# Sums over channels of a LayerNorm in four 32-column groups, with smaller edits at the start and in a scan

## What is computed

```python
# first block, at its very start: the modulation of the input from c
mod = jnp.dot(jax.nn.silu(c), w_mod[l]) + b_mod[l]          # 1 x 6144
h = rms_norm(x, g_norm1[l]) * (1.0 + scale1) + shift1
proj = jnp.dot(h, w_in[l])

# second block, Conformer branch: a LayerNorm over 1024 channels
u = causal_depthwise_conv(u, conf_conv_w[i], conf_conv_b[i])   # 31 taps
u = jax.nn.silu(layer_norm(u, conf_ln_g[i], conf_ln_b[i]))
y_conf = u * jax.nn.silu(cgate)

# second block, state-space branch: a scan over chunks of 128 tokens
def step(h, inp):
    s, d = inp                     # d: decay of the chunk
    return h * d[..., None, None] + s, h
```

## Time and profile before

| | |
|---|---|
| three runs | 2256.68, 2260.80, 2262.57 us; median 2260.8 |
| the profiled execution | 2260.23 us, of which its span is 2258.5 |
| busy shares of the span | PE 93%, PE weight loads 72%, DVE 76%, ACT 47%, POOL 8% |
| mean granted clock of PE | 0.96 of full speed |
| moved by DMA | 381.7 MB, mean 169 GB/s |

### The profile page before, as it was taken

One profiled execution on the slowest core, in us unless ns is written; L12 is line 12 of the kernel. 1 busy time (PEld: TensorE's weight loads), 2 busy tenths in 40 slices (PEclk: granted clock), 3 DMA queues, 4 the chain that ended last, 5 costly groups with the idle time before them and its releaser, 6 DMA issues. The chain is left out here.

```text
span 2258.5 us, 24881 instructions
## 1 busy us (share of the span) xinstructions
PE 2095.7 (93%) x9816; PEld 1619.0 (72%) x9816; DVE 1710.6 (76%) x1731; ACT 1064.4 (47%) x1213; POOL 178.5 (8%) x152
## 2 busy tenths in 40 slices
PE   5999998999945999999999869999999988899998
PEld 3766844777834888888888557888888764588876
DVE  4565248895566899999999469999999858883776
ACT  4288134883214777777777322113132156524043
POOL 2000010000000011111111200000000000024040
PEclk8999998999967999999999979999999998999999
DMA  9111161002286899999998931121123143253111
GB/s 335 48 38 38 38 240 55 1 1 86 112 318 237 314 402 394 398 397 393 402 393 310 291 123 40 66 80 42 47 86 136 40 165 124 81 194 127 38 66 66
DMA packets 130014, 381.71 MB, mean 169 GB/s; under 512 B 10579, under 2 KB 21099, under 8 KB 129920
## 3 DMA queue, kind: packets, MB, share of 16 engines
q1 hardware_dynamic: 115104, 340.41, 39.6%
q0 software_dynamic: 7568, 23.09, 4.0%
q10 hardware_dynamic: 7248, 16.93, 1.9%
HBM read 337.28 MB, written 43.06 MB: 168 GB/s over the span
## 5 line engine op out<-in xcount | busy, mean ns | idle before, releaser
L2269 DVE SCALAR_TENSOR_TENSOR arena<-arena,vecs 128x1023 f32<-128x1023 f32 (+14 forms) x240 | 304.3, 1268 | 7.1
L1702 DVE TENSOR_TENSOR w_low<-W,w_high 128x2048 fp32r<-128x2048 f32 x96 | 216.9, 2286 | 38.8 <-ACT w_high L1647 38.8
L1971 PE MATMUL Q<-hT_high,w_high 128*128 128x512 f32 (+1 forms) x736 | 230.7, 393 | 1.3 <-PEq L1991 1.3
L1702 DVE TENSOR_TENSOR w_low<-arena,w_high 128x2048 fp32r<-128x2048 f32 x96 | 218.3, 2289 | 17.4 <-ACT w_high L1647 17.4
L1647 ACT ACTIVATE w_high<-W 128x2048 fp32r<-128x2048 f32 x96 | 184.0, 1919 | 96.1 <-PE Q L1577 65.2
L1971 PE MATMUL Q<-hT_low,w_high 128*128 128x512 f32 (+1 forms) x720 | 225.4, 391 | 0.0
L1971 PE MATMUL Q<-hT_high,ring_low 128*128 128x512 f32 x704 | 220.6, 391 | 0.0
L1647 ACT ACTIVATE w_high<-arena 128x2048 fp32r<-128x2048 f32 x96 | 184.2, 1920 | 74.5 <-PE Q L1577 74.5
L1577 PE MATMUL Q<-w_high,x_high 128*128 128x512 f32 x512 | 160.6, 395 | 2.4 <-DVE x_low L1705 2.4
L1984 ACT ACTIVATE w_high<-W 128x1024 fp32r<-128x1024 f32 x44 | 46.4, 1057 | 244.4 <-PE Q L1971 242.0
L1971 PEld LDWEIGHTS Q<-hT_high,w_high 128*128 128x128 f32 (+1 forms) x736 | 136.0, 185 | 34.1 <-issue 2.4
(11 more groups left out here) (449 smaller groups left out, 4160.2 us busy)
## 6 DMA issues: line engine op xcount, KB each, us to landing
W<-in_w_dram SPq DMA_DIRECT2D x48, 2048.0 KB, 13.3
arena<-in_w_dram SPq DMA_DIRECT2D x48, 2048.0 KB, 12.1
W<-in_w_mod_dram SPq DMA_DIRECT2D x12, 2048.0 KB, 15.7
W<-in_w_in_dram SPq DMA_DIRECT2D x12, 2048.0 KB, 9.1
W<-in_w_out_dram SPq DMA_DIRECT2D x6, 2048.0 KB, 9.9
spill<-arena ACTq DMA_DIRECT2D x24, 512.0 KB, 2.6
W<-in_w_in_dram SPq DMA_DIRECT2D x8, 1024.0 KB, 8.7
W<-cs_rows SPq DMA_DIRECT2D x11, 512.0 KB, 3.6
```

What stands on the lines that cost most here:

```text
L1702: nc.vector.tensor_tensor(wl[:], chunk_src(r, j), wh[:].bitcast(F32), ALU.subtract).then_inc(low_v, 1)
L1971: ins = nc.tensor.matmul(Q[rows, 2 * pair_of(n) + half, :], w[:, k], x[:, k, HALF * half:HALF * half + HALF], start=k == 0 and w is high a ...
L2269: ins = nc.vector.scalar_tensor_tensor(conf[:, i, j:], u[:, 0:S - j], w, conf[:, i, j:], ALU.mult, ALU.add)
```

## The change

1. c is loaded as 8 rows of 128 beside the other rows; one transpose of 32 rows (in the place of 24) turns all into columns and comes ahead of the product of unit 0. ACT reads c's columns from PSUM for the silu. `small_loads` moves from the first block's POOL list to that of the next block. The 16 matmuls that make columns are cut into four groups of four, each behind the product of the unit after.
2. `mean` and `var` become two entries each. Entry 0: 16 matmuls of 32 columns of ones, tile k to the 32-partition group k mod 4, so each group holds the sum over two tiles. ACT copies the pair to SBUF (`group_part`). Entry 1: two matmuls (one for each half) with the full ones, which add the groups; every group holds its sum 32 times, so the scales are 1/(32 * 1024). The mean moves behind z4, the variance behind z5. The squares get eight buffers instead of two, and no wait for PE.
3. `decay_of(i)` has four places, and waits for the update of step i-4.
4. xs is loaded in three DMAs of 128, 384 and 512 tokens; PE waits for the second at chunk 1 and for the third at chunk 4.

```diff
-                act.dma_start(c_col, A["c"][0].rearrange("(k p) -> p k", p=P), allow_slow_non_contiguous=True).then_inc(c_in, 16)
+                act.dma_start(row_stack[3 * KD:], A["c"][0].rearrange("(k p) -> k p", p=P)).then_inc(row_in, 16)
...
-                act.wait_ge(c_in, 16)
-                nc.scalar.activation(silu_c, c_col, ACT.Silu).then_inc(c_ready, 1)
+                act.wait_ge(row_tr, 1)
+                nc.scalar.activation(silu_c, Q[:, 7, 3 * KD:4 * KD], ACT.Silu).then_inc(c_ready, 1)
...
+                def turn_part(u):
+                    pe.wait_ge(mod_copied, u + 1)
+                    for j in range(4 * u, 4 * u + 4):
...
-                pe.wait_ge(row_in, 32)
+                pe.wait_ge(row_in, 48)
+                nc.tensor.transpose(Q[:, 7, 0:4 * KD], row_stack, ident[0:4 * KD, 0:4 * KD]).then_inc(row_tr, 1)
...
                     mod_product(pe, unit(pe, u), 4 + u % 2)
+                    turn_part(u - 1)
+                turn_part(3).then_inc(cols_mm, 1)
...
-        order.insert(order.index(("z", 4)), ("mean", 0))
-        order.insert(order.index(("z", 5)), ("var", 0))
+        at_z5 = order.index(("z", 5))
+        order[at_z5:at_z5] = [("mean", 0), ("mean", 1)]
+        at_z6 = order.index(("z", 6))
+        order[at_z6:at_z6] = [("var", 0), ("var", 1)]
...
-                for n, cols_n in enumerate((slice(0, 2 * P), slice(2 * P, S))):
+                for n, cols_n in enumerate((slice(0, P), slice(P, 4 * P), slice(4 * P, S))):
...
+                        if m == 0:
...
+                            pe.wait_ge(ready, KD)
+                            for half in range(2):
+                                for k in range(KD):
+                                    g = k % GROUPS
+                                    ins = nc.tensor.matmul(Q[P // 4 * g:P // 4 * g + P // 4, 2 * pair_of(n) + half, :],
+                                                           ones[:, 0:P // 4],
+                                                           terms[k][:, HALF * half:HALF * half + HALF],
+                                                           start=k < GROUPS, stop=k >= GROUPS)
+                        else:
+                            pe.wait_ge(in2_s, s_level[kind, 0])
...
+                                                       group_part[:, HALF * half:HALF * half + HALF],
...
-                        if k >= 2:
-                            act.wait_ge(sq_used, k - 1)
-                        nc.scalar.activation(conf_sq[k % 2], conf[:, k], ACT.Square).then_inc(sq_ready2, 1)
+                        nc.scalar.activation(conf_sq[k], conf[:, k], ACT.Square).then_inc(sq_ready2, 1)
...
+                    elif kind in ("mean", "var") and m == 0:
+                        ins = nc.scalar.activation(group_part, pair(what), ACT.Copy)
...
-                    if i >= 2:
-                        act.wait_ge(state_ready, i - 1)
+                    if i >= 4:
+                        act.wait_ge(state_ready, i - 3)
```

More of the change, by code:

```diff
@@ L187, in program @@
         skip_col = small_cols(KD)
-        chunk_decay = small_cols(2 * HPG)
+        chunk_decay = small_cols(4 * HPG)
         mv = small_cols(2)
@@ L524, in _ @@
                 send_units(sync, U_GATE1 + NU)
+            @block.gpsimd
+            def _(pool):
+                small_loads(pool)
             @block.tensor
@@ L1860, in program @@
         place = {what: n for n, what in enumerate(order)}
-        vector_reads = [w for w in order if w[0] in ("value", "mean", "turn", "bc", "xs")]
+        vector_reads = [w for w in order if w[0] in ("value", "turn", "bc", "xs") or w == ("mean", 1)]
         chunks = [w for w in order if w[0] not in ("mean", "var", "turn")]
@@ L1875, in program @@
                     act_list.append(("step", chunks[p]))
-        act_list.insert(act_list.index(("high", chunks.index(("z", 7)))), ("step", ("var", 0)))
+        at_z7 = act_list.index(("high", chunks.index(("z", 7))))
+        act_list[at_z7:at_z7] = [("step", ("mean", 0)), ("step", ("var", 0)), ("step", ("var", 1))]
         scalar_steps = [what for kind, what in act_list if kind == "step"]
@@ L1924, in program @@
         decayed = [spare2[:, 0], tiles(2), spare[:, 0]]
+        conf_sq = [tiles(0), tiles(1), tiles(3), tiles(5), tiles(37)] + [spare2[:, j] for j in (0, 2, 3)]
         cs_bc = [spare2[:, 1], tiles(3), spare[:, 1]]
@@ L1932, in program @@
         grown = arena[:, 37 * 1024 + 768:37 * 1024 + 896]
-        xs_in = [sem(f"xs_in{n}") for n in range(2)]
+        xs_in = [sem(f"xs_in{n}") for n in range(3)]
         cs_in = [sem(f"cs_in{j}") for j in range(3)]
@@ L2154, in _ @@
                         continue
[L2155 to L2157 removed]
+                    if kind in ("mean", "var"):
+                        if m == 0:
+                            terms, ready = ([conf[:, k] for k in range(KD)], conf_ready) if kind == "mean" else \
+                                (conf_sq, sq_ready2)
+                            pe.wait_ge(ready, KD)
[8 more added lines that the diff above has]
+                            pe.wait_ge(in2_s, s_level[kind, 0])
                             for half in range(2):
                                 ins = nc.tensor.matmul(Q[:, 2 * pair_of(n) + half, :], ones[:],
[L2160 to L2165, removed]
[L2166 to L2172 removed]
+                                                       group_part[:, HALF * half:HALF * half + HALF],
+                                                       start=True, stop=True)
                         ins.then_inc(in2_mm, 1)
@@ L2256, in _ @@
                         act.dma_start(spill[slot_of[kind] + m], stage[i % 2]).then_inc(stage_out[i % 2], 16)
-                    if what == ("z", 3):
+                    if what == ("mean", 0):
                         squares()
```

49 lines of the change are left out of this document (17 added, 32 removed).

## The result

| | before | with the change |
|---|---|---|
| five runs each | 2256.68 to 2267.97, median 2262.57 us | 2239.83 to 2245.62, median 2241.97 us |
| the profiled execution | 2260.23 us (span 2258.5) | 2245.62 us (span 2243.9) |
| mean granted clock of PE | 0.96 | 0.963 |

The ratio is 0.9915, 95% interval [0.9898, 0.9933]: 19 us faster, between 15 and 23.

The account below looks back on a forecast made before the run. PE, busy for 93% of the span, was taken to bound the kernel. Start 4.7, norm 7.0 and scan 0 sum to 11.7 us: 2248.5 against the profiled 2260.23, forecast 2249.0 for the runs' median, range 2243.5 to 2256.0.

Parts of the forecast that it names:

- narrow matmuls take what weight products do: At the norm's mean and var: 16 narrow matmuls side by side take 3.44 us, as two weight products do.
- The lower clock behind the wait ahead of z7: At the norm: after PE waits 4.1 us, 1.2 GHz for about as long, losing 2.0 us; bounds nothing and 10.9.
- Step 1 of the scan still waits for its sums: At the scan's start: ACT's step 1 waits for sums behind xs, landing 19.6 us after its issue as before.
- start: First block: faster transfers and cut column matmuls start the next block earlier, at 43.5 for 48.33; gain 4.7 us.
- norm: Mean through z7: cheaper sums end z7 9.0 us earlier, less 2.0 for lower clock; gain 7.0 us.
- scan, xs: Scan: four decay places 0, bound 1.9 us; three xs loads 0, between 3.1 lost and 3.0 gained.
- 2.4 lay between var's end and the reciprocal: At the norm: this gap kept, var ending at 1816.3 puts the reciprocal at 1818.7, and PE waits 4.1 us.
- The gain is thus between 3.3 and 4.8; I take **4.7: At the start: next block at 43.5 for 48.33, its first unit there by 45.0 at the latest; 4.7 us taken.
- The range: Whole kernel: 2243.5 to 2256.0 us, leaving out the top of "more than summed" and the last three rivals.
- more than summed: Rival, 14%: clock stays up (2.0), sums come early (up to 3.0), scan gains up to 1.9; 2242 to 2246.
- The two slow rivals of the clock: At the norm: z7 wholly at half clock, 2257.9 (5%); or z5 to z7 at half clock, 2279.8 (4%).
- The rule that I weighed and left: Start and norm: tiling changes drain TensorE, nine drains costing 1.8 us, sum 9.9 for 11.7; not used.

Follow-up runs that it names:

- e1: The start's edits alone (c as rows, POOL's small loads in the next block, column matmuls cut in four) on the kernel before; ratio 0.9970, 6.8 us faster.
- e3_scan_only: Four places for the decay factors and xs in three DMAs, alone on the kernel before (also written e3); ratio 1.0000, 0 us faster.
- e2: The norm's edits alone (group sums with a combining product, mean behind z4, variance behind z5, eight square buffers) on the kernel before; ratio 0.9962, 8.6 us faster.
- e12: The kernel before with nothing but the three loads of xs and PE's waits with it; ratio 0.9994 [0.9983, 1.0005].
- e4: The whole change once more, beside its parts on one chip, against the kernel before; ratio 0.9926, 16.7 us faster.
- e10: The whole change a third time, unaltered, against the kernel before; ratio 0.9918, 18.5 us faster.
- e9: The changed kernel with all 16 column matmuls behind the last product again; ratio to the kernel before 0.9921 [0.9906, 0.9936].
- e6: The changed kernel with the sums of scan step 1 sent ahead of xs, into their own place; ratio to the kernel before 0.9929, 16.0 us faster.
- e8: The changed kernel with POOL's 18 small loads back in the first block, c still rows; ratio to the kernel before 0.9944 [0.9926, 0.9962].
- e5: The changed kernel with z7's low part made right behind that of z6; ratio to the kernel before 0.9925, 17.0 us faster.
- e7: The changed kernel with z7's low part early and step 1's sums ahead of xs; ratio to the kernel before 0.9893, 24.2 us faster.
- e11: Repeat of the changed kernel with z7's low part early and step 1's sums ahead of xs; ratio to the kernel before 0.9910, 20.3 us faster.

## Why the prediction was wrong

**What held.** The direction, the places and the mechanisms. x is held up by small pieces, product 0 comes early (8.90; about 9 to 10 forecast), narrow matmuls take what weight products do (3.64 for 3.44). In the times of before (the changed kernel is 4.09 us ahead at the last convolved tile), z5 starts at 1798.12 for 1798.1 forecast, z6 at 1815.81 for 1815.7. The lower clock behind the wait ahead of z7 was forecast at 2.0 us and cost 1.6. Step 1 of the scan still waits for its sums, the scan's turn of two steps is as long as before (12.34 us), and the scan is worth 0 by its own run.

**What was mis-sized.**

| term | forecast | traces | runs |
|---|---|---|---|
| start | 4.7 | 5.65 (5.4 in e1) | 6.8 (4.3 to 9.0) |
| norm | 7.0 | 8.35 | 8.6 (5.2 to 11.8) |
| scan, xs | 0 | 2.2 behind the issue of xs | 0 (-2.3 to 2.5) |
| given back before the norm | 0 | -1.56 | |
| sum | 11.7 | 14.6 | 19.2, 16.7, 18.5 |

- *The norm's step that failed* is "2.4 lay between var's end and the reciprocal". I carried these 2.4 us over from before whole. 1.28 of them was ACT's table load for the root, which before stood behind the sums, with nothing beside it (ACT's timeline of before):

```profile
1818.45 1.28 ACT L2246 ACT_TABLE_LOAD   x1 [0.39 <-ACT arena L2237]
1819.75 1.12 ACT L2246 ACTIVATE arena<-Q,small 128x1024 f32<-128x1024 f32 x1
```

  With a copy of the pair ahead of the full matmuls, ACT loads the table while PE adds the groups (1810.20 beside 1810.33 above). So the reciprocal starts 1.1 us earlier than forecast, PE waits 2.80 and not 4.1, and z7's low part is there 1.0 us earlier. That is most of the 1.35 that the norm gives above the forecast; the other 0.3 is the clock, which cost less than I had put.
- *The start's step that failed* is "The gain is thus between 3.3 and 4.8; I take **4.7**". x came 3.6 us earlier and not 3.3, since the changed stretch runs at 407 and not at 391 GB/s (9 x (407 - 246)/407 = 3.6), and product 1 with it 3.8; and 0.87 of the row of 4.60 that I counted as work was lower clock in that one execution. I gave the cutting of the matmuls a gain that belongs to the split of the wait, and left out the 0.45 us that the cutting costs. By the trace of e3_scan_only as before, the start's gain is 4.4 us and inside my bounds, so this step is shown wrong against one trace only; by its own run it is worth 6.8 us (4.3 to 9.0), and this interval holds the forecast.
- *The scan's 2.2 us* behind the issue of xs does not come from its edits: e2, which has none of them, has it too (404.95 us to the end, 407.3 before), and e3, which has nothing else, doesn't (407.4). Over all executions with the norm's edit as it is, it is 404.4 to 406.1 us; without it 405.1 (e12) to 407.4. These overlap, so an effect of the norm's edit isn't shown either, and its cause stays open. What of it is the sums' landing (18.1 to 19.8 us behind the issue of xs, with either form of xs) and what the clock in the scan's first 20 us was not tried apart.
- *The range.* Its low end stood 5.5 us below the forecast. The two mis-sized terms and the 2.2, less the 1.56, make up the profile's 14.6 us; the rest to the first result's 20.6 between the medians I put down to draws: the profiled execution of the change was 3.65 us above its median, and before's was 2.3 below the median of its five runs, which itself lies above the medians of 2260 to 2261 of later runs. The changed kernel's medians of 2243.94 (e4) and 2243.57 (e10) lie 0.4 and 0.1 us inside the range, so that the first one lay outside it is partly luck. The sum of 11.7 us is short all the same: the three timings gave 19.2, 16.7 and 18.5. That all three lie above the traces' 14.6 is not explained. A range for a kernel whose own runs spread over 6 us has to hold that spread, and mine held the costs' bounds alone.

The rival "more than summed" (2242 to 2246) was the right case by size and wrong by its reasons: the clock did not stay up in the profiled execution (in others it did, see the last section), the sums did not come early, and four decay places gave nothing. The two slow rivals of the clock did not come: z5 and z6 ran at full rate. The rule that I weighed and left, that a change of tiling mode drains TensorE (the Trainium skill, TensorEngine Tiling (Array Packing), Key Properties), would have cost 1.8 us by my estimate. At the norm the trace shows none of it: the narrow matmuls of var follow z5 without an idle time (1805.45), and z5 and z6 start on the forecast to 0.1 us. At the start it may be part of the 0.45 us that four more changes cost (e9), 0.1 us each and not 0.2; whether that is a drain no run here shows.

## What to carry to other kernels

When a step is moved, look at what stood inside each gap that you carry over: a table load in it leaves the path once its engine has earlier work to hang it on. Before a wait of PE is removed, look at which engine ends the block, and list everything that PE's end releases: here DVE's chain ended the block already, and xs's transfers, released earlier, met cg's. Where two waits end side by side, test them together before calling either worthless. And size a stretch by several traces, since one execution's lower clock looks like work: a stretch that no edit touched took 1742.9 to 1755.5 us in three executions of one kernel.

## What the runs showed of the hardware

**The same wait, with and without a fall of the clock.** I had read from before that the clock stays at its upper level (2.4 GHz) behind 2.8 us of idle PE and is at the lower (1.2 GHz) behind 3.6. The norm of the change has a wait of 1.98 us ahead of the mean and one of 2.8 ahead of z7, and its executions show all four outcomes. The granted clock was 1.00 ahead of both waits in each of them. The rows are the mean's narrow matmuls in e6 and in e4, and the stretch behind the wait ahead of z7 in e6:

```profile
1788.76 3.64 PE L2174 MATMUL Q<-arena,ones 128*32 128x512 f32 x32 [1.98 <-DVE arena L2280]
```

```profile
1785.61 5.32 PE L2172 MATMUL Q<-arena,ones 128*32 128x512 f32 x32 [1.98 <-DVE arena L2278]
```

```profile
1826.90:1831.90 5.00, 4.94 (x22) 4.11 (x23) 5.00 (x5) 5.00 (x5) 0.00 (x0) 1.00 0.10 39
```

| execution | mean's narrow matmuls | behind z7's wait | first narrow matmul to xs |
|---|---|---|---|
| e6 | 3.64 us, clock up | up (1.00) | 49.39 us |
| first profile of the change | 3.64, up | down (0.66) | 50.96 |
| e2, e9, e10 | 5.34, down | up | 51.03 to 51.05 |
| e4, e8 | 5.32 and 5.34, down | down | 52.67, 52.68 |

The wait ahead of z7 is gone in e5, e7 and e11; their narrow matmuls took 3.64, 3.64 and 5.34 us. Each fall costs 1.6 to 1.7 us. With the same instructions and the same waits to 0.03 us, the clock fell or not; so the length of the wait right in front doesn't decide it alone, and what else does is open. For a forecast it is a draw, between 6.6 and 9.9 us for the norm here.
